# Rotary partners of the first attention: VectorE shuffles in place of TensorE rotations

## What is computed

```
q, k, v = split(h @ w_qkv)              # 8 heads, each with 2 components of 64 for q and k, v of 128
q, k = partial_rope(q), partial_rope(k)  # the first 16 of each 64: t1*c - t2*s, t1*s + t2*c, rest as it is
s = q k^T / 8, causal mask, softmax, for each component
a = p[component 0] - lam * p[component 1]
o = rms_norm(a @ v) ; out = o @ w_o
```

## Time and profile before

| | before |
|---|---|
| runs, us | 1466.49, 1468.98, 1465.28; median 1466.49 |
| span of the profiled execution, us | 1468.2 |
| mean granted PE clock, share of full | 0.998 |
| busy: PE / DVE / ACT / POOL | 98% / 72% / 48% / 2% |
| instructions in the trace | 28465 |
| HBM read | 266.73 MB, 182 GB/s over the span |

### The profile page before, as it was taken

One profiled execution on the slowest core, in us unless ns is written; L12 is line 12 of the kernel. 1 busy time (PEld: TensorE's weight loads), 2 busy tenths in 40 slices (PEclk: granted clock), 3 DMA queues, 4 the chain that ended last, 5 costly groups with the idle time before them and its releaser, 6 DMA issues. The chain is left out here.

```text
span 1468.2 us, 28465 instructions
## 1 busy us (share of the span) xinstructions
PE 1446.1 (98%) x11585; PEld 1406.6 (96%) x11585; DVE 1056.6 (72%) x1439; ACT 700.0 (48%) x910; POOL 29.0 (2%) x58
## 2 busy tenths in 40 slices
PE   8999999999999999999999999999999999999999
PEld 8999999999999999999999889999987899999999
DVE  6766779777667786677878768767887777876652
ACT  6544353454443454443554655443436766544431
POOL 0000100000001000001000000001000000000000
PEclk9999999999999999999999999999999999999999
DMA  9555835437447644458343226647633436365540
GB/s 324 220 187 186 268 149 201 172 106 267 172 172 249 239 173 172 171 196 288 128 173 124 78 70 246 227 173 268 234 115 135 145 139 231 131 228 185 184 173 30
DMA packets 42538, 269.09 MB, mean 183 GB/s; under 512 B 4768, under 2 KB 5920, under 8 KB 13520
## 3 DMA queue, kind: packets, MB, share of 16 engines
q1 hardware_dynamic: 33984, 240.31, 45.1%
q0 software_dynamic: 7312, 26.44, 5.5%
q10 hardware_dynamic: 1152, 1.05, 0.2%
HBM read 266.73 MB, written 1.05 MB: 182 GB/s over the span
## 5 line engine op out<-in xcount | busy, mean ns | idle before, releaser
L418 PE MATMUL ps<-x_hi,w_hi 128*128 128x272 f32 (+2 forms) x2296 | 661.8, 288 | 6.7 <-DVE x_lo L1447 1.9
L420 PE MATMUL ps<-x_hi,w_lo 128*128 128x272 f32 (+2 forms) x2296 | 651.8, 284 | 0.0
L419 PE MATMUL ps<-x_lo,w_hi 128*128 128x272 f32 (+2 forms) x2296 | 651.7, 284 | 0.0
L2024 ACT ACTIVATE w_hi<-raw_weights 128x2048 fp32r<-128x2048 f32 x219 | 416.9, 1912 | 291.6 <-PE ps L420 289.0
L1174 DVE TENSOR_TENSOR w_lo<-raw_weights,w_hi 128x2048 fp32r<-128x2048 f32 x193 | 439.7, 2288 | 143.8 <-ACT w_hi L2024 143.3
L418 PEld LDWEIGHTS ps<-x_hi,w_hi 128*128 128x128 f32 x2296 | 433.1, 189 | 10.8 <-DVE x_lo L1380 2.5
L419 PEld LDWEIGHTS ps<-x_lo,w_hi 128*128 128x128 f32 x2296 | 433.3, 189 | 0.7
L420 PEld LDWEIGHTS ps<-x_hi,w_lo 128*128 128x128 f32 x2296 | 433.1, 189 | 0.0
L418 PE MATMUL ps<-a_hi,w_hi 128*128 128x272 f32 x592 | 169.6, 286 | 0.0
L419 PE MATMUL ps<-a_lo,w_hi 128*128 128x272 f32 x592 | 169.6, 286 | 0.0
L420 PE MATMUL ps<-a_hi,w_lo 128*128 128x272 f32 x592 | 169.6, 286 | 0.0
(11 more groups left out here) (259 smaller groups left out, 1543.9 us busy)
## 6 DMA issues: line engine op xcount, KB each, us to landing
raw_weights<-w_units SPq DMA_DIRECT2D x226, 1024.0 KB, 4.9
mod_w<-mod_units POOLq DMA_DIRECT2D x48, 512.0 KB, 5.5
raw_weights<-w_units SPq DMA_DIRECT2D x4, 256.0 KB, 5.8
raw_weights<-w_units SPq DMA_DIRECT2D x2, 512.0 KB, 9.2
out<-h ACTq DMA_DIRECT2D x8, 128.0 KB, 1.9
h<-x_in SPq DMA_DIRECT2D x2, 272.0 KB, 4.1
h<-x_in SPq DMA_DIRECT2D x1, 544.0 KB, 8.0
tab<-tables POOLq DMA_DIRECT2D x1, 512.0 KB, 7.9
```

The source lines that it names most:

```text
L418: pe.matmul(dst, wh, hi, start=start, stop=False)
L419: pe.matmul(dst, wh, lo, start=False, stop=False)
L420: return pe.matmul(dst, wl, hi, start=False, stop=stop)
L2024: act.activation(w_hi[:, u % RING, :], raw[:, u % RING, :], ACT.Copy).then_inc(S["hi_ready"], 1)
```

## The change

1. PE no longer does any `rot`. On DVE, `partners` shuffles partitions within blocks of 32: partition i takes i + 8, i + 8 takes i, the others stay. It takes both query tiles of a group (j = 0) or both key tiles (j = 1) in one instruction of 544 columns, into f. `rope` then works on a pair of tiles too: product with sin1, product with cos1, sum.
2. The signs move into the table: `signed_sines`, once before the first eviction, sums the rows of rot1 and multiplies sin1 by minus that sum.
3. `scores` waits for all four tiles of its group (`4 * g + 4`).
4. In the DVE list the half splits, shuffles and rotations are put in another order. In the first group: signs, eviction of the queries, shuffle, eviction of the keys, rotation of the queries, half split, shuffle, half split, rotation of the keys, two half splits. In the last group a half split leaves its place between the maximum of step 11 and `subln(1)` and comes after `subln_lo(1)`; the rotation of the queries comes ahead of the last eviction.
5. On PE, behind the projection, the rotations go; `early_slab(1)` comes ahead of `scores(12)`, `early_slab(2)` ahead of `scores(13)` and `early_slab(3)` ahead of `turn_p(12)`.

```diff
+PARTNERS = [i + 8 if i < 8 else i - 8 if i < 16 else i for i in range(32)]
...
-            def rot(g, m, bank=7):
...
             def scores(s):
...
-                pe.wait_ge(S["qk_ready"], 4 * g + 2 + 2 * j)
+                pe.wait_ge(S["qk_ready"], 4 * g + 4)
...
-            second_group(qkv, 2, {
-                1: [lambda: rot(0, 0)], 2: [lambda: rot(0, 2)], 3: [lambda: rot(0, 1)], 4: [lambda: rot(0, 3)],
-                7: [lambda: scores(0)]})
+            second_group(qkv, 2, {7: [lambda: scores(0)]})
...
-                1: [lambda: rot(1, 0)], 2: [lambda: rot(1, 2)], 3: [lambda: rot(1, 1)],
-                4: [lambda: rot(1, 3), lambda: scores(4)],
+                4: [lambda: scores(4)],
...
-                1: [lambda: values(5), lambda: rot(2, 0)],
-                2: [lambda: scores(7), lambda: turn_p(6), lambda: rot(2, 2)],
-                3: [lambda: values(6), lambda: rot(2, 1)],
-                4: [lambda: turn_p(7), lambda: rot(2, 3)],
+                1: [lambda: values(5)],
+                2: [lambda: scores(7), lambda: turn_p(6)],
+                3: [lambda: values(6)],
+                4: [lambda: turn_p(7)],
...
-            rot(3, 0)
             values(11)
-            rot(3, 2, bank=4)
             early_slab(0)
             subln_sums(1, range(4), last=3)
-            pe.wait_ge(S["rotation_read"], 14)
+            early_slab(1)
             scores(12)
-            rot(3, 1)
-            early_slab(1)
-            rot(3, 3)
+            early_slab(2)
             scores(13)
-            early_slab(2)
+            early_slab(3)
             turn_p(12)
-            early_slab(3)
             values(12)
...
+            def signed_sines():
+
+                dve.wait_ge(rope1_loaded, 32)
+                chain(dve.tensor_reduce(lam[:, 6:7], rot1, AX.X, ALU.add))
+                chain(dve.tensor_scalar(sin1, sin1, lam[:, 6:7], -1.0, ALU.mult, ALU.mult))
+
+            def partners(g, j):
+
+                if g and j == 0:
+                    dve.wait_ge(S["qk_ready"], 4 * g)
+                dve.stream_shuffle(f[:, 4 + 2 * j:6 + 2 * j, :], qk1[:, g % 2, 2 * j:2 * j + 2, :], PARTNERS)\
+                   .then_inc(S["vec_chain"], 1)
+                return c.up("vec_chain")
+
+            def rope(g, j, shuffled):
+
+                x, turned = qk1[:, g % 2, 2 * j:2 * j + 2, :], f[:, 4 + 2 * j:6 + 2 * j, :]
+                dve.wait_ge(S["vec_chain"], shuffled)
+                dve.tensor_tensor(turned, turned, bcast(sin1, TOK), ALU.mult).then_inc(S["vec_chain"], 1)
+                dve.tensor_tensor(x, x, bcast(cos1, TOK), ALU.mult).then_inc(S["vec_chain"], 1)
+                dve.wait_ge(S["vec_chain"], c.up("vec_chain", 2))
+                dve.tensor_tensor(x, x, turned, ALU.add).then_inc(S["qk_ready"], 2)
...
-            evict_qk(0)
-            low_half()
-            rope(0, 0)
-            low_half()
-            rope(0, 2)
-            rope(0, 1)
-            low_half()
-            rope(0, 3)
+            signed_sines()
+            evict_qk(0, (0,))
+            at = partners(0, 0)
+            evict_qk(0, (1,))
+            rope(0, 0, at)
+            low_half()
+            at = partners(0, 1)
+            low_half()
+            rope(0, 1, at)
+            low_half()
             low_half()
 
             evict4(qkv, V_GROUP[0], v1_T[:, :, :], TOK, True)
...
             combine(3)
+            at = partners(1, 0)
             low_half()
             evict_qk(1, (1,))
 
-            low_half()
-            low_half()
-            rope(1, 0)
-            low_half()
-            rope(1, 2)
-            rope(1, 1)
-            rope(1, 3)
+            rope(1, 0, at)
+            low_half()
+            at = partners(1, 1)
+            low_half()
+            rope(1, 1, at)
+            low_half()
             peak(4)
...
             peak(6)
-            rope(2, 0)
+            at = [partners(2, j) for j in range(2)]
             combine(6)
             low_half()
             peak(7)
-            rope(2, 2)
+            rope(2, 0, at[0])
             combine(7)
-            rope(2, 1)
-            low_half()
-            rope(2, 3)
+            rope(2, 1, at[1])
+            low_half()
             low_half()
...
             peak(11)
-            low_half()
+            at = partners(3, 0)
             subln(1)
             combine(11)
             subln_lo(0)
+            rope(3, 0, at)
 
             evict_qk(3, (1,))
-            rope(3, 0)
-            rope(3, 2, bank=4)
+            rope(3, 1, partners(3, 1))
             subln_lo(1)
+            low_half()
             peak(12)
             head_roots(0, 3)
-            rope(3, 1)
             combine(12)
             low_half()
             peak(13)
-            rope(3, 3)
             combine(13)
```

## The result

The changed kernel takes 1472.60 us (median of 20 runs, 1467.47 to 1477.34); the kernel before, run beside it 20 times, takes 1469.91 (1465.28 to 1473.82). The ratio is 1.0025, with an interval of [1.0015, 1.0035]: slower by 0.25%, inside the 0.3% that I had called "no change", but outside my range, which ended at 1470.1. Two things are in that miss from the start. The median of three runs that I started from, 1466.49, was itself low; all 141 runs of the kernel before in this study have a mean of 1470.0. And the change costs 2.7 us where my sum had a gain of 0.8. One execution of the kernel before took 2383.67 us at a granted clock of 0.55 and is left out of every number here.

The account below looks back on a forecast made before the run. PE, busy 98%, bounds the kernel, but 7.4 of the 8.2 us taken from it return as waits for DVE: +0.2 - 0.85 - 1.05 + 0.9 = -0.8 us, from 1466.5 to 1465.7; range 1462.2 to 1470.1.

Parts of the forecast that it names:

- my sum: Over the qkv projection and first attention: +0.2 - 0.85 - 1.05 + 0.9 = -0.8 us, giving 1465.7; chance 0.46.
- What bounds the kernel: PE is busy 98% of the span, but gains depend on how far DVE lies behind where PE waits.
- the price of what is removed: Sixteen rotations leaving PE in the projection: 1.39 + 15 x 0.455 = 8.2 us, the most the edit can give.
- the price on DVE: A group costs DVE 5.5 us instead of 5.0: shuffle 0.64, a pair's rotation 2.11; signs 0.79 once.
- (d): A dearer shuffle, twice in each of four waits, makes the kernel slower; at 1.4 us each, 1471.8; chance 0.07.
- Groups 0, 3 and 4: PE's waits for DVE in the projection: 2.9 us ahead of group 2, 0.95 before scores(4), 0.75 before turn_p(7).
- The last group: At the end of the projection and behind it, DVE's order makes PE wait, giving back two rotations and +0.9 us.
- (a): TensorE's clock falls in the new gap before group 2, costing 1.7 us: 1467.4; chance 0.26.
- a dip at 753: PE's clock dipping behind the new gap before group 2, which would show that the clock fall there is real.
- (b): PE runs nowhere into DVE and keeps all 8.2 us: 1458.3; chance 0.06.
- (c): A shuffle of 0.36 us in the four waits (1463.5), or no loss at the projection's end (1464.8); together 0.15.

Follow-up runs that it names:

- experiment 5: The changed kernel with DVE's order rewritten in all four groups, weight halves that can wait put behind awaited work: 1466.10 us, ratio 0.9976; run again, 1466.13, ratio 0.9983.
- experiment 7: Three more profiled runs of the unchanged changed kernel, 1477.18, 1475.76 and 1475.26 us, and the kernel with all DVE orders rewritten once more, 1466.13 us.
- experiment 4: The changed kernel with only DVE's order at the end of the stage put back as in the kernel before: 1470.29 us, ratio 1.0004.
- calm_before: The kernel before, with DVE in the down stages splitting the next weight piece ahead of the modulation that waits for mod_w: 1471.00 us, ratio 1.0016.
- hole_before: The kernel before with five needless DVE multiplications ahead of group 0's V eviction, so that PE waits there: 1476.71 us, ratio 1.0037.

## Why the prediction was wrong

**What bounds the kernel, the price of what is removed, and the price on DVE: right.** The 32 matmuls went, and the shuffle, which no row showed and on which the slower rival (d) hung, came within 0.02 us of the row with its width. My estimate from the Trainium skill's rate for it (VectorE: DVE Perf Modes, the perf-mode tier table) had given the same 0.64, and the trace, with 0.66, agrees.

**Groups 0, 3 and 4: right in place and size. The last group: right in size, its reason not borne out.** Waits of 2.80, 0.98 and 0.84 against 2.9, 0.95 and 0.75. The sum of -0.8 came out as -0.4. Up to the last matmul of the projection 1.5 us were saved, for a forecast of 1.7 (828.62 - 722.17 = 106.45 before, 827.26 - 722.34 = 104.92 after); behind it 1.1 were lost, for a forecast of 0.9. But I had put that loss down to the order on DVE, and with the order put back only 0.1 of it came back.

**The step that failed: my own sum put the clock's cost behind the new gap at nothing, and took 0.46 for it against 0.26 for rival (a), which I priced at 1.7 us.** I had argued for (a) from the fall behind 867.62 and against it from a wait of 0.69 at 741 that cost no clock; but the new gap is over three times as long as that one and belonged with the other. The fall comes in two thirds of the profiles and mostly takes 3.4 us, twice the 1.7 that I had read off one fall. So (a) was the truth, and its price was 2.1 us by the profiles, 2.8 by the clock of all executions. The sign that I had given for it, a dip at 753, was not in the first profile and is in three of the five of the changed kernel. The Trainium skill (TensorE: Matmul & The Clock Gate, Part 1) has the gate pass half the pulses after an idle stretch. The half agrees with the granted clock of 0.50 in these six; in the other three the same gap of 2.26 us cost nothing, so here the fall is a chance and no certainty. What decides it I haven't found.

**The base: three runs.** My forecast hung on their median, 1466.49, and I took the profiled run's distance from it for spread within 3.7 us. The kernel's executions in fact lie between 1464.7 and 1476.2, and the mean of 141 is 1470.0. Of the miss of 6.9 us (1472.6 against 1465.7) 3.4 are this base (1469.91 beside the changed kernel, for 1466.49), some 2.8 the clock and 0.4 the stage; 0.3 are left, less than the noise.

**The other rivals.** (b), that PE takes it all, failed for the reason given: the order of bank reuse. But experiment 5 shows how much of it was to be had in the stage, 4.9 of 8.2 us, mostly by moving weight halves that I had counted as given; the whole gained 2.5 to 3.5. (c) and (d) did not occur. Where the 0.7 us fall that lie between the 2.1 by the profiles and the 2.8 by all executions was not shown; chance alone made a difference of 1.2 between the two sets of profiles ahead of the change.

## What to carry to other kernels

Work taken from the bounding engine is worth only what the helping engine's order lets through: list, at each wait, what stands in that engine's queue ahead of the awaited instruction and isn't itself awaited, and move that behind. Price a new gap of TensorE not by its length alone: here 2.3 us of waiting lost on average 2 to 3 more at half clock, and needless matmuls in the gap brought the clock loss from 7.2 to 5.2 without shortening it (a gain in time from them is not shown). And for effects under 0.3%, take the base from dozens of runs, and compare stretch by stretch between matmuls common to both kernels: the stage's length, where no fall came into it, repeated within 0.1 us (123.5 three times, 123.1 to 123.2, 118.5 to 118.6), where the whole moved by 10.

## What was not expected of the hardware

**The clock fell inside the gap, and at chance.** In the first of the three profiles of experiment 7 the gap ends at 754.56, and the clock is down before that, with PE idle:

```profile
753.50:754.00 0.50, 0.00 (x0) 0.00 (x0) 0.50 (x2) 0.00 (x0) 0.00 (x0) 0.82 0.36 148
754.00:754.50 0.50, 0.00 (x0) 0.00 (x0) 0.50 (x2) 0.00 (x0) 0.00 (x0) 0.50 0.00 0
```

So it is in all six profiles with the fall, earliest in that of experiment 4 (0.64 from 751 to 754). In three it never falls, with the same wait of 2.26 us.

**TensorE has two paces at full clock.** The stage behind, up(3), runs the same matmuls in all kernels. In the kernel before, in the version of 5, and in the latter's second run, from 900 to 980:

```profile
900.00:980.00 80.00, 80.00 (x708) 80.00 (x708) 56.54 (x48) 39.24 (x32) 0.00 (x0) 1.00 0.57 209
```
```profile
900.00:980.00 80.00, 80.00 (x681) 80.00 (x680) 54.60 (x44) 36.30 (x29) 0.00 (x0) 1.00 0.53 188
```
```profile
900.00:980.00 80.00, 80.00 (x708) 80.00 (x707) 56.37 (x46) 38.06 (x30) 0.00 (x0) 1.00 0.55 205
```

At a clock of 1.00 and with PE busy throughout, 708 matmuls are 113 ns each, 681 are 117.5. The version of 5 kept the slow pace from 885 to 1060 in its first profile, which for its 1475 matmuls comes to an estimated 6.5 us, and had the fast one there for most of its second. The two differ by 6.3 us behind the stage (627.8 and 621.5), though the second lost more to the clock. `calm_before` and `hole_before` had the slow one too, and others changed from fast to slow in between, near 1000. So it goes with neither kernel, and it may make a good part of the spread of 10 us between executions of one program, which these few profiles don't prove. What sets it stayed open; it was not tried.
